# Stick-breaking attention scores as stacked fp32r products in a streaming-encoder block

## What is computed

```python
def _stick_breaking(q, k, v):          # 8 heads of 64, strictly causal
    ...
        z = jnp.einsum('bhqd,bhkd->bhqk', qi, kf) * scale
        mask = s_idx[None, :] < t_idx[:, None]
        log_keep = jnp.where(mask, jax.nn.log_sigmoid(-z), 0.0)
        suffix = lax.cumsum(log_keep, axis=3, reverse=True) - log_keep
        a = jnp.where(mask, jnp.exp(jax.nn.log_sigmoid(z) + suffix), 0.0)
        return jnp.einsum('bhqk,bhkd->bhqd', a, vf)
```

## Time and profile before

| | |
|---|---|
| median of 3 runs | 1464.25 us (1463.91 to 1464.27) |
| profiled execution | 1466.18 us, span 1464.5 us, granted clock 0.999 |
| TensorE matmul busy | 1455.2 us, 99% of the span |
| TensorE weight load busy | 1208.1 us, 82% |
| VectorE busy | 1107.4 us, 76% |
| ScalarE busy | 747.2 us, 51% |
| GpSimd busy | 424.6 us, 29% |
| chain that ended last | TensorE 86%, VectorE 10%, ScalarE 2%, GpSimd 1% |

### The profile page before, as it was taken

The page is one execution under the profiler, slowest core; times in us unless marked ns, Lnnn a source line. Parts: engine busy times, 40 slices in busy tenths (PEclk is TensorE's granted clock), DMA queues, the critical chain, the costliest instruction groups (busy, mean ns, idle before and its releaser), DMA issues.

```text
span 1464.5 us, 22288 instructions
## 1 busy us (share of the span) xinstructions
PE 1455.2 (99%) x7466; PEld 1208.1 (82%) x7466; DVE 1107.4 (76%) x1903; ACT 747.2 (51%) x955; POOL 424.6 (29%) x200
## 2 busy tenths in 40 slices
PE   9999999999999999999999999999999999999999
PEld 8888777878788888888888888888888888888887
DVE  5977688867589999996999997346666666666665
ACT  6444677477645454554556555454444444444442
POOL 5866435436546687884000000000000000000000
PEclk9999999999999999999999999999999999999999
DMA  7544533538433666666888888988888888888883
GB/s 239 172 144 144 202 123 108 174 121 300 152 116 115 219 219 208 215 209 206 299 304 303 310 297 305 321 285 287 297 297 281 296 283 296 284 293 286 292 286 139
DMA packets 166705, 345.16 MB, mean 236 GB/s; under 512 B 13420, under 2 KB 78956, under 8 KB 164336
## 3 DMA queue, kind: packets, MB, share of 16 engines
q1 hardware_dynamic: 166640, 344.32, 69.2%
HBM read 268.76 MB, written 75.51 MB: 235 GB/s over the span
## 4 chain that ended last, share of the span: by engine, by line
PE 86%; DVE 10%; ACT 2%; POOL 1%; issue 0%; DMA 0%; SPq 0%; ACTq 0%; POOLq 0%
PE ps L1229 32%; PE ps L1220 25%; PE ps L747 9%; PE ps L770 6%; PE ps L1258 4%; PE ps L1089 3%; DVE top_lists L2156 1%; DVE top_lists L2149 1%; POOL u_r L538 1%; PE ps L954 1%; PE ps L735 1%; DVE top_in L2150 1%; DVE top_lists L2153 1%; DVE top_lists L2146 1%; PE ps L938 1%; PE ps L964 1%
## 5 line engine op out<-in xcount | busy, mean ns | idle before, releaser
L1220 PE MATMUL ps<-hT_r,u_r 128*128 128x512 f32 x2048 | 470.6, 391 | 0.1
L1229 PE MATMUL ps<-v_r,w_pairs 128*128 128x512 f32 x2036 | 461.7, 389 | 0.0
L1220 PEld LDWEIGHTS ps<-hT_r,u_r 128*128 128x128 f32 x2048 | 382.8, 188 | 79.7 <-POOL u_r L538 0.5
L1229 PEld LDWEIGHTS ps<-v_r,w_pairs 128*128 128x128 f32 x2036 | 382.3, 188 | 79.2
L491 POOL TENSOR_TENSOR w_r<-w_raw,w_r 128x1024 fp32r<-128x1024 f32 x85 | 217.0, 2558 | 182.5 <-ACT w_r L1337 105.0
L2295 DVE TENSOR_TENSOR v_r<-vraw,v_r 128x1024 fp32r<-128x1024 f32 x128 | 156.9, 1226 | 148.7 <-ACT v_r L1675 148.7
L1675 ACT ACTIVATE v_r<-vraw 128x1024 fp32r<-128x1024 f32 x128 | 135.7, 1061 | 253.6 <-PE ps L1229 249.0
L1622 ACT ACTIVATE act_stage<-ps 128x512 f32<-128x512 f32 x128 | 76.6, 598 | 226.5 <-PE ps L1220 226.4
L538 POOL TENSOR_TENSOR u_r<-uraw,u_r 128x1024 fp32r<-128x1024 f32 x60 | 172.9, 2892 | 46.6 <-ACT u_r L1603 46.4
L1337 ACT ACTIVATE w_r<-w_raw 128x1024 fp32r<-128x1024 f32 x95 | 100.0, 1059 | 112.2 <-PE ps L747 44.9
L1603 ACT ACTIVATE u_r<-uraw 128x1024 fp32r<-128x1024 f32 x128 | 134.9, 1054 | 15.8 <-DMA uraw<-in_u 12.9
(11 more groups left out here) (272 smaller groups left out, 1538.6 us busy)
## 6 DMA issues: line engine op xcount, KB each, us to landing
uraw<-in_u SPq DMA_DIRECT2D x128, 512.0 KB, 4.8
vraw<-in_v SPq DMA_DIRECT2D x128, 512.0 KB, 5.2
w_raw<-in_w SPq DMA_DIRECT2D x100, 512.0 KB, 3.5
acts_out<-act_stage SPq DMA_DIRECT2D x128, 256.0 KB, 2.3
gates<-stage SPq DMA_DIRECT2D x16, 2048.0 KB, 7.4
g_in<-gates SPq DMA_DIRECT2D x64, 512.0 KB, 6.4
act_in<-acts_out SPq DMA_DIRECT2D x128, 256.0 KB, 5.2
gates_pre<-pre_stage SPq DMA_DIRECT2D x24, 256.0 KB, 2.4
```

The costliest lines, as they stand in the source:

```text
L1220: ins = pe.matmul(bank(s % 2), u2[s][:, w, k * P:(k + 1) * P], hr4[:, w, k, :], start=i == 0, stop=i == 15, skip_group_check=True)
L1229: ins = pe.matmul(bank(2 * q + h), w2[:, s, w, q * P:(q + 1) * P], v2[s][:, w, h * BANK:(h + 1) * BANK], start=start and w == 0, stop=stop ...
```

## The change

The scores of a head become one set of fp32r products over all 128 partitions: the key's high part (64 rows) and low part (64 rows) are stacked, and the query's in the same way, so that one product adds both. `stacks[p]` has four tiles of 128x512 for pair p: query and key of the first head, query and key of the second. ScalarE writes the high parts into the head's own 64 partitions (`stack_high`), VectorE the low parts into the other 64 (`stack_low`): all four of pairs 0 and 1, only the queries (i = 0 and 2) of pairs 2 and 3. GpSimd writes the low parts of the keys (i = 1 and 3) of pairs 2 and 3 (`stack_key`). Queries in `projT` are scaled by SPREAD more. The tiles lie in space that `y_sbT` and `r_all` use later, so the broadcast to `r_all` moves from gate 1 to gate 13 on SP, behind a wait for the fourth pair's scores. Some semaphores are merged.

```diff
+        of_y, of_r = ([s[:, i * T:(i + 1) * T] for i in range(4)] for s in (stack_y, stack_r))
+        stacks = [of_y, of_r, of_y[1:] + [stack_x], of_r]
...
@@ gpsimd
-            low_ws(I_G + GATES_IN_KV, 14)
+            def stack_key(p, i):
+                wait_low_w(pool, I_G + GATES_IN_KV + 3 * p - 3)
+                at_least(pool, stack_lo_pool, 2 * p - 4 + i // 2)
+                pool.wait_ge(stack_hi, 4 * p + i + 1)
+                h, s = half(i // 2), stacks[p][i]
+                pool.tensor_tensor(s[half(1 - i // 2), :], projT3[h, 4 + p, :], s[h, :].bitcast(F32),
+                                   ALU.subtract).then_inc(stack_lo_pool, 1)
+            low_ws(I_G + GATES_IN_KV, 4)
+            for p in range(2):
+                for i in (1, 3):
+                    stack_key(p + 2, i)
+                pool.wait_ge(stack_lo_pool, 2 * p + 2)
+                low_ws(I_G + GATES_IN_KV + 4 + 3 * p, 3)
+            low_ws(I_G + GATES_IN_KV + 10, 4)
@@ sync, in the loop over gates
-                if m == 1:
+                if m == GATES_IN_KV + 3 * (PAIRS - 1):
+                    sp.wait_ge(z_ready, PAIRS)
                     sp.wait_ge(row_out, 48)
                     sp.dma_start(r_all, acts_dram[0, 0:4, :].rearrange("h t -> (h t)").partition_broadcast(P)
@@ tensor
             def sb_scores(p):
                 at_least(pe, a_ready, 2 * p)
+                pe.wait_ge(stack_lo, (4, 8, 10, 12)[p])
+                if p >= 2:
+                    pe.wait_ge(stack_lo_pool, 2 * p - 2)
                 for kt in range(TT):
                     for h in range(2):
-                        pe.matmul(causal(h, kt), projT3[half(h), 4 + p, kt * P:(kt + 1) * P],
-                                  projT3[half(h), p, kt * P:T], start=kt != 3, stop=False, skip_group_check=True)
+                        query, key = stacks[p][2 * h:2 * h + 2]
+                        pe.matmul(causal(h, kt), key[:, kt * P:(kt + 1) * P], query[:, kt * P:T],
+                                  start=kt != 3, stop=False, skip_group_check=True)
@@ scalar
+            def stack_high(p, i):
+                h, s = half(i // 2), stacks[p][i]
+                act.activation(s[h, :], projT3[h, i % 2 * 4 + p, :], ACT.Copy,
+                               scale=(1.0 / SPREAD, KEEP)[i % 2]).then_inc(stack_hi, 1)
@@ in the natural-layout items
+                    if b == 2:
+                        stack_high(0, j)
@@ in the memory-value items
+                if n < I_KV + 6:
+                    stack_high(1, n - I_KV - 2)
@@ in the pairs
                 exp_part(2 * p)
+                if p < 2:
+                    stack_high(p + 2, 0)
+                    stack_high(p + 2, 1)
                 exp_part(2 * p + 1)
+                if p < 2:
+                    stack_high(p + 2, 2)
+                    stack_high(p + 2, 3)
@@ vector
+            def stack_low(p, i):
+                h, s = half(i // 2), stacks[p][i]
+                dve.wait_ge(stack_hi, 4 * p + i + 1)
+                if i % 2:
+                    ins = dve.tensor_tensor(s[half(1 - i // 2), :], projT3[h, 4 + p, :], s[h, :].bitcast(F32), ALU.subtract)
+                else:
+                    ins = dve.scalar_tensor_tensor(out=s[half(1 - i // 2), :], in0=s[h, :].bitcast(F32), scalar=1.0 - SPREAD,
+                                                   in1=projT3[h, p, :], op0=ALU.mult, op1=ALU.add)
+                ins.then_inc(stack_lo, 1)
@@ behind natural-layout block 2
+                elif b == 2:
+                    for i in range(4):
+                        stack_low(0, i)
@@ behind gate 2
+            for i in range(2):
+                stack_low(1, i)
             dve.wait_ge(item_done, V_AT[3] + 1)
...
+            for i in range(2, 4):
+                stack_low(1, i)
             take_gate(3)
@@ in the pairs, behind take_gate(m + 1)
+                if p == 0:
+                    stack_low(2, 0)
+                    stack_low(2, 2)
                 if 1 <= p < PAIRS - 1:
                     split_low(p - 1)
+                    stack_low(3, 2 * p - 2)
                 take_gate(m + 2)
```

More of the change, by code:

```diff
@@ L211, in build @@
         pre_stage = carve("pre_stage", 5120, 1024)
+        stack_y, stack_r, stack_x = carve_r("stack_y", 38928, 2048), carve_r("stack_r", 40976, 2048), carve_r("stack_x", 2560, 512)
         y_ml = carve("y_ml", 40976, 2048)
@@ L286, in build, with half @@
         yT = [y.rearrange("p (g t) -> p g t", t=T) for y in (y_sbT, y_mlT, y_memT)]
+        of_y, of_r = ([s[:, i * T:(i + 1) * T] for i in range(4)] for s in (stack_y, stack_r))
+        stacks = [of_y, of_r, of_y[1:] + [stack_x], of_r]
+        def half(h):
+            return slice(SBD * h, SBD * h + SBD)
         gate_s3 = gate_s.rearrange("p (s c) -> p s c", c=2 * T)
@@ L409, in build @@
         ml_split_hi, ml_split_lo = sem("ml_split_hi"), sem("ml_split_lo")
+        stack_hi, stack_lo, stack_lo_pool = sem("stack_hi"), sem("stack_lo"), sem("stack_lo_pool")
         s_ready, d_ready, e_ready, e_masked, w_ready, num_done, num_out = (
@@ L412, in build @@
             sem("num_out"))
-        ml_squared, ml_factors, ml_normed, mlT_done, mlT_out = (
-            sem("ml_squared"), sem("ml_factors"), sem("ml_normed"), sem("mlT_done"), sem("mlT_out"))
+        ml_factors, ml_normed, mlT_done, mlT_out = (
+            sem("ml_factors"), sem("ml_normed"), sem("mlT_done"), sem("mlT_out"))
         qkT_done, qkT_out = sem("qkT_done"), sem("qkT_out")
@@ L908, in turn_rows @@
             def turn_rows():
-                pe.wait_ge(thr_made, 1)
+                pe.wait_ge(if_made, 2)
                 pe.wait_ge(y_out, PAIRS - 1)
@@ L1403, in _ @@
             high_w(I_N + 2, (I_N + 2) % 4)
-            act.activation(r_abs, r_abs, ACT.Ln, bias=1.0).then_inc(if_ln, 1)
+            act.activation(r_abs, r_abs, ACT.Ln, bias=1.0).then_inc(if_made, 1)
             for b in range(4):
@@ L1411, in _ @@
                         silu(SILU_AFTER[b, j])
+                    if (b, j) == (1, 3):
+                        act.wait_ge(proj_out, NT)
+                    if b == 2:
+                        stack_high(0, j)
+            act.wait_ge(rows_made, 1)
             for n in range(I_KV + 2, I_G + GATES_IN_KV):
                 high_w(n, n % 4)
-            act.wait_ge(qk_squared, 2)
+                if n < I_KV + 6:
+                    stack_high(1, n - I_KV - 2)
+            act.wait_ge(squared, 3)
             act.activation(roots[:, S_Q:S_ML], sums[:, S_Q:S_ML], ACT.Sqrt, bias=eps_col[:, :],
-                           scale=1.0 / HD).then_inc(qk_rooted, 1)
+                           scale=1.0 / HD).then_inc(rooted, 1)
             high_w(I_G + 4, (I_G + 4) % 4)
@@ L1463, in _ @@
                     act.wait_ge(rows_made, 1)
-                    act.activation(r_m, r_m, ACT.Exp, scale=-1.0).then_inc(thr_made, 1)
+                    act.activation(r_m, r_m, ACT.Exp, scale=-1.0).then_inc(if_made, 1)
                 if p < PAIRS - 1:
@@ L1786, in _ @@
                 if g < 4:
-                    dve.scalar_tensor_tensor(out=projT3[:, g, :], in0=bank(t_bank(j)), scalar=SBD ** -0.5, in1=rstd_b,
+                    dve.scalar_tensor_tensor(out=projT3[:, g, :], in0=bank(t_bank(j)), scalar=SBD ** -0.5 * SPREAD, in1=rstd_b,
                                              op0=ALU.mult, op1=ALU.mult).then_inc(proj_out, 1)
@@ L1803, in _ @@
             dve.tensor_tensor(r_max, bank(0)[0:MLH, :], rstd_b[0:MLH, :], ALU.mult).then_inc(if_rows, 1)
-            dve.wait_ge(if_ln, 1)
+            dve.wait_ge(if_made, 1)
             link(dve.tensor_scalar(r_f, r_zero, bif[:, 1:2], 0.0, ALU.add, ALU.min))
@@ L1855, in norm_q @@
             def norm_q():
-                dve.wait_ge(qk_rooted, 1)
+                dve.wait_ge(rooted, 3)
                 link(dve.reciprocal(rstd[:, S_Q:S_ML], roots[:, S_Q:S_ML]))
@@ L1983, in _ @@
             dve.tensor_reduce(sums[:, S_ML:S_H], squares.rearrange("p (g c) -> p g c", c=HD), AX.X,
-                              ALU.add).then_inc(ml_squared, 1)
+                              ALU.add).then_inc(squared, 1)
             def gate_ml():
```

13 lines of the change are left out of this document (5 added, 8 removed).

## The result

| | before | changed |
|---|---|---|
| median | 1464.61 us | 1468.23 us |
| lowest to highest | 1463.86 to 1466.86 | 1465.47 to 1470.06 |
| ratio of the times | | 1.0023, 95% interval 1.0016 to 1.0030 |
| profiled execution, span | 1464.5 us | 1465.9 us |

The changed kernel is 3.6 us slower, just over the 0.2% (2.9 us) that the prediction took as the bound; the interval has this bound inside it. The median is within the stated range (1460 to 1468.3) by 0.07 us, but the forecast was no change, 1464.8. The runs also scatter more than those of before. The changed kernel's profiled execution (1467.65 us) is one of its shorter ones, and that of before (1466.18 us) one of the longer.

What follows compares the result with a forecast made beforehand. TensorE's chain through the attention stage was taken to bound the kernel. Pair shifts of +1.37, −1.11, +0.65 and −0.3 summed to +0.6 us on the median 1464.25, so 1464.8 us (no change, 0.55); range 1460 to 1468.3.

Steps and rivals of the forecast that it cites:

- The saving: Score products of each of four pairs: 1.25 us in place of 2.36, 4.44 us in all.
- the 4.27 that the prediction works out for four passes: A pair's old scores, if true fp32 took four passes of every column at 2.4 GHz: 4.27 us, saving some 12.
- The turns at the interface: VectorE operations with two SBUF inputs and GpSimd's weight products alternate by whole instructions; new VectorE operations 1.8 to 3 us.
- Whoever has waited goes next: Rule for VectorE and GpSimd at SBUF: after each whole instruction, the engine that has waited runs next.
- Pair 0: Low parts and GpSimd's weights delay taking gate 3, so gate 4 starts near 170.8; +1.37 us in place of −1.11.
- the moved broadcast: r_all's broadcast, from gate 1 to 13, lands before decay(0); weights 45 and 46 land earlier, worth nothing alone.
- Pair 1: Low query parts fit where VectorE idled ahead of gate 6; saving kept, −1.11 us, sum +0.26.
- The 0.48 us in hand: Slack of the low part in pair 1's suffixes, which covers a 0.3 us later second Exp.
- Pair 2: GpSimd's key part goes before stack_low(3, 0), gate 9 is taken late, TensorE waits 1.7 to 1.8 us: +0.65.
- Pair 3: If VectorE keeps the interface, stack_low(3, 2) is 0.7 to 0.8 us late for the scores: −0.3, sum +0.6 us.
- The case that I gave 0.2: Slower rival: GpSimd's weights precede stack_low(3, 2), last pair's scores 3.2 us late; sum +3.0, 1467.3 us; chance 0.2.
- ScalarE's copies and the merged semaphores: 16 ScalarE copies of 64x512, 9.9 us, hidden in its waits and costed at nothing; merged semaphores also nothing.

Runs made afterwards that it cites:

- The last experiment: The kernel of the free slots with split_low(0) moved from minus_abs(2): query half behind stack_low(3, 0), key half behind minus_abs(3); 1459.29 us, ratio 0.9964.
- the yielding GpSimd: Changed kernel with one more wait: GpSimd begins weights 55 only when VectorE has made all low parts of pair 3; 1464.32 us, ratio 0.9997.
- the third experiment: Changed kernel with pair 1's last two low parts behind minus_abs(0) and both pair 3 stack_low operations ahead of pair 2's splits; 1465.22 us, ratio 0.9998.
- the free slots: Changed kernel, VectorE reordered: pair 1's low parts behind memory values and minus_abs(0), mLSTM splits behind next pair's absolute value; 1460.21 us, second set 1461.11.

## Why the prediction was right and wrong

**The saving** was right: 1.25 us for a pair's scores forecast, 1.22 measured, 4.56 in all rather than 4.44. The last experiment shows all of it on TensorE, and another 0.1 us a pair. Why the old scores took 2.36 us, and not the 4.27 that the prediction works out for four passes, was not tested.

**The turns at the interface** were the right mechanism, read from the two slow splits of the earlier trace rows. The new operations took 1.3 to 2.9 us beside GpSimd and 0.7 without, and the yielding GpSimd shows cause and not only company. "Whoever has waited goes next" holds in the rows shown here, but not down to 0.01 us: in the profile of the third experiment weights 45 began at 163.31 and the second low part at 163.32, and the low part went first (0.68 us, the weights 2.96).

**Pair 0**: +1.37 forecast, +0.77 measured. The turns came as forecast (weights 45, the third low part, weights 46, the fourth), but gate 3 was taken some 0.6 us earlier, mostly because weights 45 had begun earlier: 0.99 us after the start of the gate product ahead of the first scores, not 1.75 as before. The prediction saw that the moved broadcast would let these weights land earlier and called it worth nothing. In five of the seven profiles that have pair 1's first two low parts in front of the memory's values they came earlier still, 0.45 to 0.70 us after that start, ahead of the second low part, and TensorE waited 1.36 us for the memory's values. The forecast took that order into account for gate 3, and left out that it makes TensorE wait ahead of the scores as well. Where gate 3 is taken behind all four low parts, the profiles with that wait need 21.38 to 21.44 us to gate 6, the changed kernel's own 21.04, so it was lucky by 0.4 us.

**Pair 1**: −1.11 forecast, −1.25 measured. The 0.48 us in hand sufficed.

**Pair 2**: +0.65 forecast, −0.10 measured. The order of turns was right: GpSimd's key part asked at 205.28, waited behind the second split (ended at 205.75) and ended near 206.9, and `stack_low(3, 0)` then ended at 207.44. The sum was wrong. Its own terms (207.43 + 0.26 + 1.2 + 0.68 + 0.69) take gate 9 at about 210.3 and not 210.6, and TensorE wants gate 10 at 210.00 + 0.26 − 1.11 = 209.15 and not 208.95. That is a wait of about 1.1 us rather than 1.7 to 1.8, and 0.93 was measured.

**Pair 3** is the step that failed: "If VectorE keeps the interface, ... 0.8 − 1.11 = −0.3". GpSimd had it, by 0.02 us. I had read 228.04 and 228.05 from the trace of before and taken the side that led by 0.01. The changed kernel's profile has the same two times, 226.26 for the end of the split and 226.27 for the start of the weights; what I left out is that `stack_low(3, 2)` starts 0.03 us after the split's end. Nor was it chance: in the four profiles that keep this order (the changed kernel, pair 1's last low parts moved, TensorE kept busy, GpSimd's part undone) weights 55 began 0.02 or 0.03 us ahead each time. The case that I gave 0.2 was the one that happened. It had 3.2 us of lateness, and 3.14 was measured. A near tie like this should not have been settled by 0.01 us, and the dear side (3.2 us against 0.8) should have carried more of the forecast.

**The clock** was in no case. The prediction took every wait at its own length. The 3.14 us wait cost 4.8 in the profile, and the runs scatter up to 4.6 us above the lowest, mostly the longer ones with the lower mean clock. With pairs 0 and 2 together 1.35 us better than forecast (0.60 and 0.75), the rival's +3.0 would have been some +1.6; the measured +3.6 has the clock in it. That the rival's 1467.3 comes within 1 us of the median is therefore luck: waits taken too long in pairs 0 and 2, and the clock, which no case had, pull in opposite directions.

**ScalarE's copies and the merged semaphores** cost nothing in this stage, as forecast; the last experiment has them, and the full saving. The broadcast costs nothing there either, but in the changed kernel's order it moves weights 45 among the low parts, as told for pair 0. In the profile, 0.5 us of pair 3's loss comes back in the branch stage (317.48 to 361.55 before, 319.42 to 362.99 now). Why was not followed.

## What to carry to other kernels

When an operation of VectorE with two SBUF inputs is added, look at what GpSimd runs at that minute: its price is up to one whole GpSimd instruction, and where several stand ahead of something that TensorE waits for, count them against the GpSimd instructions in the way. The same work in another order was worth between 8 and 9 us here (ratios to before of 1.0023 and 0.9964). A tie between two engines' requests is to be priced at the bad end, or removed by a wait on the engine that has time.

## What the runs showed of the hardware that I had not expected

A hole of 3.14 us on TensorE brought a mean granted clock of 0.72 in the stretch from 228 to 234, and 1.64 us more than the hole itself; filled with 13 products, the same wait brought none. The profiles with the same wait agree: behind 3.13 us (pair 1's last low parts moved) the scores took 1.77 us, and behind 3.79 us (GpSimd's part undone) 1.71 us with a mean clock of 0.72 from 234 to 240. The holes of 2.95 us (GpSimd's part undone, ahead of gate 10), 2.34 us and 2.16 us were followed by a clock of 1.00. These are single executions, and no run tells what would happen to the same hole in another.

The 19 runs of the kernels of the free slots and of the last hole, which have no hole over 1 us there, list 1.000 (12 runs) or 0.999 (7). But not every low mean clock comes from a hole of this stage: the kernel before, with no hole over 0.22 us there, lists 0.999 in many runs and 0.998 in two, and its own profile has 0.83 from 10 to 20 us. This is also why the two spans (1464.5 and 1465.9) differ by 1.4 us where the medians differ by 3.6: the profile of before has 1.20 us of it at the start and 0.5 in the branch stage, and the attention stage alone differs by 3.13.
